# The passage to the experts in another order, with the difference of the first token tile on GpSimd

## The chip, the cores and the metric

The kernel runs on one NeuronCore of a Trainium2 chip. The metric is the device time of one launch in microseconds (us); for the kernel before it is the median of three runs. In the profile PE is TensorE (matmuls; PEld its weight loads), DVE is VectorE, ACT is ScalarE, POOL is GpSimd, and SP is the engine that issues most DMAs.

## What is computed

One layer of an encoder on 256 tokens (and 16 meta tokens) of width 2048, all in float32. The first sub-layer mixes latent attention and retention. The second is a mixture of experts, and the change lies at the passage between the two:

```python
h = layer_norm(ALPHA * h + mix, ln1_g, ln1_b)
g_sel = argmax(h @ w_group + b_group)                     # one of 4 groups
e_local = top_k(e_logits[g_sel] + e_bias, 2)              # two of its 8 experts
e_w = softmax(chosen e_logits) * softmax(g_logits)[g_sel]
y = (silu(x @ w1[e]) * (x @ w3[e])) @ w2[e]               # 32 experts, 512 wide
h = layer_norm(ALPHA * h + sum over the two of e_w * y, ln2_g, ln2_b)
```

## The kernel before

**Precision.** TensorE multiplies float32 at full rate only in a rounded form (float32r). So each operand is kept as a rounded high part and a low part that holds the difference. ScalarE copies a piece of weights (`raw`) to its high part `wh`, VectorE subtracts and writes `wl`. A *unit* is 1 MB of weights (128 partitions by 2048 columns), and the expert weights are 384 units: 12 for each of 32 experts (4 each of w1, w3 and w2). Units x = 10 and 22 of each pair of experts are used unsplit in four-pass float32 (`XR`, line 286).

**Stream of weights.** SP issues the loads into a ring of eight slots (`load`, line 436). The load of unit n waits until TensorE has used unit n - 8. Units 0 to 7 are loaded in the first sub-layer; unit 8 is the first whose load waits for an expert unit.

**The expert loop.** Experts are taken in pairs, 24 steps k to a pair. The first pair leaves out k = 4 to 7 (`body` and `step`, lines 422 to 428), so that its steps are k = 0 to 3 and 8 to 23; its unit at k = 14 is the unsplit one, x = 10. At each step every engine does its part for the unit and then small tasks bound to certain k: ScalarE evicts (`copy_up`, `outputs`, `gathered`), VectorE selects (`select`), builds the next gather matrix and the hidden products, TensorE folds hidden products (`mix`, line 1010, at k = 12, which waits for `s_pd` of `select`). Four gathers of the next pair follow the units k = 8 to 11 of the first pair (`G_FIRST`).

**The passage.** The normalised stream `mrg` (two token tiles t, each 128 tokens by 2048) is split into `xh1` (ScalarE, line 644) and `xl1` (VectorE, `stream_rest`, line 682), and in both the columns are permuted by a strided read, 16 elements apart. `xl1` lies over `yt`, which the router's logits (TensorE, line 2157, banks 0 and 1) read until `s_lg`. From the logits VectorE finds the assignment in some 30 small operations, each waiting for the one before (lines 712 to 733, helper `first_max`). TensorE computes ranks from it (lines 953 to 956), VectorE adds them up to `rk_`, builds the gather matrix `pg` (line 742) and a maximum (`s_mxr`, line 753). TensorE then gathers the tokens of the first two experts: for each of eight blocks q of two column groups, and for the high and the low part h, it multiplies the token tile by `pg` into a PSUM bank (`first_gather`, line 973), and ScalarE evicts each block to `xg` (`gathered`, line 555), in the order of q and after `s_gt` counts q + 1. The units of the first expert need two more blocks at each step.

Between the parts TensorE is fed with idle matmuls (`keep_warm`, line 944): 36 behind the logits, 16 behind the ranks. VectorE's order is written out: assignment, `stream_rest(0)`, ranks, gather matrix, maximum, `stream_rest(1)`, the splits of units 0 to 3 (line 755), then the first pair. At k = 3 VectorE runs all of `combine_weights` (line 758) and ScalarE the exponentials for it (`weights_exp`, line 633); `select` of the first pair is at k = 8. TensorE gathers the high parts of blocks 0 to 5 and the low parts of 0 to 3 ahead of unit 0, blocks 4 and 5 (low part) ahead of k = 1, and blocks 6 and 7 ahead of k = 2, for which banks 7 and 6 must have been evicted.

GpSimd computes inverse roots (line 1768), issues the constants' DMAs, and in the expert loop the scatters of results (`scatter`, line 521), which go through its queue.

Of the kernel before, what the change touches and what calls it, by code (L numbers as in the profile page):

```python
# [5 lines left out]
F32 = mybir.dt.float32  # L6
# [12 lines left out]
TT = SEQ // P  # L19
# [72 lines left out]
def moe_trunk(nc, ins, out):  # L92
# [15 lines left out]
    with ctx:  # L108
# [252 lines left out]
        s_xh1 = sem("s_xh1")  # L361
        s_xl1 = sem("s_xl1")
        s_lg = sem("s_lg")
# [66 lines left out]
        G_AT = (4, 6, 8, 10, 16, 18, 20, 22)  # L430
        FIRST_BANK = (7, 6, 5, 4, 3, 2, 7, 6)
        G_FIRST = (8, 9, 10, 11, 16, 18, 20, 22)
# [87 lines left out]
        def pool_experts(pool):  # L520
            def scatter(filled, par):

                pool.wait_ge(s_h1, TT)
                pool.wait_ge(s_ye[par], filled)
                pool.indirect_dma_start(yscr[:, :], bass.IndirectOffsetOnAxis(dest[0:SLOTS, par:par + 1], 0),  # L525
                                        yall[0:SLOTS, par, :], None, bounds_check=SCRATCH_ROWS - 1,
                                        oob_is_err=False).then_inc(s_scat[par], 16)

            def pairs(first, end):
                with pool.Fori(first, end) as p:  # L530
                    scatter(p, 0)
                    scatter(p, 1)

            pairs(1, PAIRS + 1)
            pool.wait_ge(s_nx, 1)
            more = pool.value_load(nxi[0:1, 0:1], min_val=0, max_val=ROUNDS - 1)
            with pool.If(more > 0):
                pairs(PAIRS + 1, PAIRS * (more + 1) + 1)
            for par in range(2):
                pool.wait_ge(s_scat[par], 16 * PAIRS * (more + 1))  # L540
            nc.gpsimd.tensor_tensor(marks[:, 5:6], half[:, 0:1], half[:, 0:1], ALU.mult).then_inc(s_all, 1)

        def scalar_experts(act):
# [46 lines left out]
            def pair(turn, par, first=False, early=None, last=False):  # L590
                for x in body(first):
# [5 lines left out]
                    hi(turn, x + HELD)  # L597
                    if k == 3 and early:
                        early()
# [62 lines left out]
        def vector_experts(dve, own):  # L662
# [19 lines left out]
            def stream_rest(t):  # L682

                dve.wait_ge(s_xh1, t + 1)
                nc.vector.tensor_tensor(xl1[:, t, :, :], mrg[:, t, :].rearrange("q (p k) -> q k p", k=KD),
                                        xh1[:, t, :, :].bitcast(F32), ALU.subtract).then_inc(s_xl1, 1)

# [46 lines left out]
            dve.wait_ge(s_asg, 1)  # L734
            stream_rest(0)
            own.after(nc.vector.tensor_scalar(r1[:, :, :], asg[:, :, :], -1000.0, 1000.0, ALU.mult, ALU.add))
# [20 lines left out]

            def combine_weights():

# [7 lines left out]
                nc.vector.tensor_tensor(ex[:, :, 0], rs[:, 10:12], rs[:, 14:16], ALU.subtract)  # L767
                nc.vector.tensor_tensor(ex[:, :, 1], rs[:, 12:14], rs[:, 14:16], ALU.subtract).then_inc(s_r1, 1)

                dve.wait_ge(s_mxt, 1)  # L770
# [75 lines left out]
            def pair(turn, p, first=False, early=None, last=False):  # L846
                for x in body(first):
                    k = step(x, first)
                    if k == (8 if first else 5):
                        select(turn, p)  # L850
# [5 lines left out]
                    lo(turn, x + HELD)  # L856
                    if k == 3 and early:
                        early()
                    if k == 0 and not first:
# [20 lines left out]

            one_round(0, 1, early=combine_weights)
            dve.wait_ge(s_nx, 1)
# [57 lines left out]
        def tensor_experts(pe, turn_stream, logits):  # L940
# [8 lines left out]
            for j in range(4):  # L949
                logits(j)  # L950
            keep_warm(36)

# [19 lines left out]

            def first_gather(q, h):

                bank = ps[:, FIRST_BANK[q], :].rearrange("p (k a h s) -> p k a h s", k=2, a=2, h=2)
                for b in range(2):
                    for t in range(TT):
                        m = nc.tensor.matmul(bank[:, b, :, h, :], (xh1, xl1)[h][:, t, 2 * q + b, :],
                                             pg[:, t, :].rearrange("p (a s) -> p a s", a=2),
                                             start=t == 0, stop=t == 1, skip_group_check=True)  # L980
                if h:
                    m.then_inc(s_gt, 1)
# [44 lines left out]
            def pair(turn, par, first=False, early=False, last=False):  # L1027
                for x in body(first):
                    k = step(x, first)
                    j = 2 * turn  # L1030
                    if early and k < 4:
                        if k == 1:
                            first_gather(4, 1)
                            first_gather(5, 1)
                        if k == 2:
                            for q in (6, 7):
                                pe.wait_ge(s_xg, q - 5)
                                first_gather(q, 0)
                                first_gather(q, 1)
                        pe.wait_ge(s_xg, 2 * k + 2)  # L1040
                    elif k == 0:
                        pe.wait_ge(s_xg, 8 * turn + 8)
# [58 lines left out]

            keep_warm(16)
            pe.wait_ge(s_pg, 1)
            pe.wait_ge(s_mxr, 1)
            pe.wait_ge(s_xh1, TT)
            for q in range(6):
                first_gather(q, 0)
            pe.wait_ge(s_xl1, TT)
            for q in range(4):
                first_gather(q, 1)  # L1110
            one_round(0, early=True)
# [1147 lines left out]
```

## Time and profile before

| | |
|---|---|
| median of 3 runs | 2149.41 us (2149.09 to 2151.28) |
| profiled execution, span from the first to the last instruction | 2148.8 us |
| median above that span | 0.6 us |
| PE, DVE, ACT, POOL busy | 96%, 74%, 59%, 5% of the span |
| HBM read | 595.05 MB |
| expert weights, loads of 1 MB by line 450 | 384 |
| mean granted TensorE clock | 0.987 |

Of the profiled execution the profile gives the span alone; what lies around it (start and end of the launch) is inside the 0.6 us by which the median stands above it. The busy shares are averages over two sub-layers with different limits. In the timeline rows below, the first number is the start in us, the second the duration, xN a merged run of N operations, and the bracket at the end the idle time of the engine before it and who ended it. A granted clock (PEclk) of 1.00 is TensorE's 2.4 GHz, 0.50 its 1.2 GHz.

### The profile page before, as it was taken

To read this page: it belongs to the slowest core of one execution; us is meant where nothing else is said; L and a number is where in the kernel's file an instruction comes from. 1 tells how busy PE (TensorE), PEld (TensorE's weight loads), DVE (VectorE), ACT (ScalarE), POOL (GpSimd) and SP (SyncE) were. 2 spreads that over 40 slices of the span, in tenths; PEclk is the share of its full clock that TensorE was granted. 3 is DMA by queue.
4 is the path that set the end of the run, shared out by engine and by line. 5 is a ranking of instruction groups with operands and counts; after the bars stand their busy time and mean duration, and the time that the engine had idled before them with its cause. 6 is when DMAs were issued, how large, how long until landed. Compare 5 with 4: busy or idle time off the path is not lost.

```text
span 2148.8 us, 30033 instructions
## 1 busy us (share of the span) xinstructions
PE 2061.8 (96%) x11484; PEld 1753.2 (82%) x11484; DVE 1596.2 (74%) x1413; ACT 1276.5 (59%) x1060; POOL 106.1 (5%) x77
## 2 busy tenths in 40 slices
PE   8999999999999999999999999999999999999992
PEld 8998888899999998887897778777777777777871
DVE  7646655453737365445668999999999999999997
ACT  5435663333233333333347888888888888888872
POOL 1000000000000000001000000000000000000001
PEclk9999999999999999999999999999999999999996
DMA  6554335655454544557747999999999999999993
GB/s 214 157 138 157 119 128 184 199 180 173 157 161 152 175 154 144 192 195 232 246 196 291 421 421 421 421 421 420 418 420 418 418 421 416 416 415 420 418 409 156
DMA packets 164607, 602.50 MB, mean 280 GB/s; under 512 B 20320, under 2 KB 28656, under 8 KB 113424
## 3 DMA queue, kind: packets, MB, share of 16 engines
q1 hardware_dynamic: 160816, 593.81, 72.7%
q0 software_dynamic: 3712, 7.59, 1.2%
q8 instruction: 55, 0.90, 0.2%
q14 instruction: 24, 0.20, 0.0%
HBM read 595.05 MB, written 18.89 MB: 286 GB/s over the span
## 4 chain that ended last, share of the span: by engine, by line
PE 66%; DVE 16%; issue 7%; DMA 7%; ACT 3%; DVEq 0%; POOLq 0%; POOL 0%; SPq 0%; ACTq 0%
PE ps L1825 19%; PE ps L1806 15%; DVE wl L692 11%; DMA raw<-in_w_dram 7%; PE ps L998 6%; PE ps L999 5%; PE ps L2177 4%; PE ps L995 3%; ACT wh L553 2%; PE ps L1020 2%; PE ps L1931 2%; PE ps L1911 2%; PE ps L1898 1%; DVE yall L843 1%; PE ps L968 1%
## 5 line engine op out<-in xcount | busy, mean ns | idle before, releaser
L692 DVE TENSOR_TENSOR wl<-raw,wh 128x2048 fp32r<-128x2048 f32 x352 | 792.0, 2288 | 42.2 <-ACT wh L553 41.1
L553 ACT ACTIVATE wh<-raw 128x2048 fp32r<-128x2048 f32 x352 | 671.1, 1916 | 140.1 <-DMA raw<-in_w_dram 83.9
L1396 DVE TENSOR_TENSOR wl<-raw,wh 128x2048 fp32r<-128x2048 f32 (+1 forms) x168 | 379.9, 2264 | 283.8 <-ACT wh L1200 283.7
L1200 ACT ACTIVATE wh<-raw 128x2048 fp32r<-128x2048 f32 (+1 forms) x168 | 318.1, 1896 | 443.7 <-DMA raw<-in_w_in_dram 282.2
L998 PE MATMUL ps<-wh,xg 128*128 128x512 f32 x900 | 376.1, 418 | 24.4 <-DVE wl L692 24.1
L999 PE MATMUL ps<-wl,xg 128*128 128x512 f32 x900 | 354.1, 393 | 0.0
L1806 PE MATMUL ps<-hth,wh 128*128 128x272 f32 (+1 forms) x896 | 259.7, 290 | 3.2 <-DVE wl L1396 1.8
L1806 PE MATMUL ps<-htl,wh 128*128 128x272 f32 (+1 forms) x896 | 255.8, 285 | 0.0
L1806 PE MATMUL ps<-hth,wl 128*128 128x272 f32 (+1 forms) x896 | 255.6, 285 | 0.0
L998 PEld LDWEIGHTS ps<-wh,xg 128*128 128x128 f32 x900 | 170.3, 189 | 77.2 <-DVE wl L692 30.3
L998 PE MATMUL ps<-wh,hx 128*128 128x512 f32 x508 | 202.0, 398 | 0.8 <-DVE wl L692 0.8
L999 PEld LDWEIGHTS ps<-wl,xg 128*128 128x128 f32 x900 | 170.5, 189 | 38.8 <-issue 7.4
L999 PE MATMUL ps<-wl,hx 128*128 128x512 f32 x508 | 198.5, 391 | 0.0
L1806 PEld LDWEIGHTS ps<-hth,wh 128*128 128x128 f32 x896 | 168.8, 188 | 5.8 <-DVE wl L1396 2.5
L1806 PEld LDWEIGHTS ps<-htl,wh 128*128 128x128 f32 x896 | 168.7, 188 | 0.3
L1806 PEld LDWEIGHTS ps<-hth,wl 128*128 128x128 f32 x896 | 168.6, 188 | 0.0
L1825 PE MATMUL ps<-wh,hth 128*128 128x512 f32 x384 | 156.1, 406 | 0.0
L1825 PE MATMUL ps<-wh,htl 128*128 128x512 f32 x384 | 151.2, 394 | 0.0
L1825 PE MATMUL ps<-wl,hth 128*128 128x512 f32 x384 | 150.8, 393 | 0.0
L525 POOL DMA_INDIRECT yscr<-yall,dest x32 | 69.4, 2170 | 942.5 <-DVE yall L843 937.9
L998 PEld LDWEIGHTS ps<-wh,hx 128*128 128x128 f32 x508 | 95.6, 188 | 20.2 <-issue 1.6
L995 PE MATMUL ps<-raw,xg 128*128 128x512 f32 x248 | 111.5, 592 | 0.0
(348 smaller groups left out, 3079.2 us busy)
## 6 DMA issues: line engine op xcount, KB each, us to landing
raw<-in_w_dram SPq DMA_DIRECT2D x384, 1024.0 KB, 10.3
raw<-in_w_in_dram SPq DMA_DIRECT2D x103, 1024.0 KB, 5.1
raw<-in_w_pa_dram SPq DMA_DIRECT2D x16, 1024.0 KB, 5.0
raw<-in_w_pb_dram SPq DMA_DIRECT2D x16, 1024.0 KB, 5.0
raw<-in_w_out_dram SPq DMA_DIRECT2D x16, 1024.0 KB, 5.0
raw<-in_w_ukv_dram SPq DMA_DIRECT2D x8, 1024.0 KB, 5.4
yrow<-yscr SPq DMA_DIRECT2D x4, 1024.0 KB, 7.8
raw<-in_w_uq_dram SPq DMA_DIRECT2D x8, 384.0 KB, 3.5
```

The costliest lines, as they stand in the source:

```text
L525: pool.indirect_dma_start(yscr[:, :], bass.IndirectOffsetOnAxis(dest[0:SLOTS, par:par + 1], 0), yall[0:SLOTS, par, :], None, bounds_check= ...
L553: nc.scalar.activation(wh2[:, x % HELD, :], raw2[:, slot2(x), :], ACT.Copy).then_inc(s_wh2, 1)
L692: nc.vector.tensor_tensor(wl2[:, slot2(x), :], raw2[:, slot2(x), :], wh2[:, x % HELD, :].bitcast(F32), ALU.subtract).then_inc(s_wl2, 1)
L995: m = nc.tensor.matmul(o, s.bitcast(F32), raw2[:, slot2(x), c:c + 512], start=st, stop=sp_, skip_group_check=True)
L998: nc.tensor.matmul(o, s, wh2[:, x % HELD, c:c + 512], start=st, stop=False, skip_group_check=True)
L999: m = nc.tensor.matmul(o, s, wl2[:, slot2(x), c:c + 512], start=False, stop=sp_, skip_group_check=True)
L1020: nc.tensor.matmul(ps[:, 6, c:c + SLOTS], ab[:, v, P * f:P * (f + 1)], fold[:, :], start=True, stop=True, skip_group_check=True)
L1200: nc.scalar.activation(wh[:, n % RING1, 0:c], raw1[:, n % RING1, 0:c], ACT.Copy).then_inc(s_wh, 1)
L1396: nc.vector.tensor_tensor(wl[:, n % RING1, 0:c], raw1[:, n % RING1, 0:c], wh[:, n % RING1, 0:c].bitcast(F32), ALU.subtract).then_inc(s_wl, 1)
L1806: m = nc.tensor.matmul(ps[:, bank, col:col + width], w[:, n % RING1, c:c + P], s[:, 4 * u + k, c0:c0 + width], start=opens and u == 0 and ...
L1825: m = nc.tensor.matmul(ps[:, bank + t, :], s[:, 4 * u + k, c:c + P], w[:, n % RING1, 512 * k:512 * (k + 1)], start=u == 0 and k == 0 and j ...
L2177: m = nc.tensor.matmul(ps[:, bank + t, :], s[:, 4 * u + k, P * t:P * (t + 1)], w[:, n % RING1, 512 * k:512 * (k + 1)], start=u == 0 and k ...
```

## The change

Five things are edited. GpSimd makes the difference of token tile 0, once the logits and the tile's high part are there, ahead of its loop of scatters; VectorE no longer does, and the semaphore `s_xl1` becomes one for each tile. The warm-up matmuls are 18 and 3 instead of 36 and 16. The first gather takes seven blocks (bank 1 joins) as one run, first all high parts, then the low parts of tile 0, then those of tile 1, and the eighth block behind them; nothing of it stays between the units. `combine_weights` is cut in two: `exponents` at k = 3 and the rest at k = 10. `select` of the first pair moves from k = 8 to k = 11, and ScalarE's exponentials from k = 3 to k = 9.

```diff
         s_yt = sem("s_yt")
         s_ytc = sem("s_ytc")
         s_xh1 = sem("s_xh1")
-        s_xl1 = sem("s_xl1")
+        s_xl1 = [sem(f"s_xl1_{t}") for t in range(TT)]
         s_lg = sem("s_lg")
         s_r1 = sem("s_r1")
         s_r2 = sem("s_r2")
@@ -428,7 +428,7 @@
             return x if first and x < 4 else x + 4
 
         G_AT = (4, 6, 8, 10, 16, 18, 20, 22)
-        FIRST_BANK = (7, 6, 5, 4, 3, 2, 7, 6)
+        FIRST_BANK = (7, 6, 5, 4, 3, 2, 1, 7)
         G_FIRST = (8, 9, 10, 11, 16, 18, 20, 22)
         LAST_BANK = (0, 1, 6, 7)
 
@@ -531,6 +531,10 @@
                     scatter(p, 0)
                     scatter(p, 1)
 
+            pool.wait_ge(s_lg, 1)
+            pool.wait_ge(s_xh1, 1)
+            nc.gpsimd.tensor_tensor(xl1[:, 0, :, :], mrg[:, 0, :].rearrange("q (p k) -> q k p", k=KD),
+                                    xh1[:, 0, :, :].bitcast(F32), ALU.subtract).then_inc(s_xl1[0], 1)
             pairs(1, PAIRS + 1)
             pool.wait_ge(s_nx, 1)
             more = pool.value_load(nxi[0:1, 0:1], min_val=0, max_val=ROUNDS - 1)
@@ -595,7 +599,7 @@
                     if k == (19 if last else 23):
                         copy_up(turn, x, 2 * turn + 1, 1)
                     hi(turn, x + HELD)
-                    if k == 3 and early:
+                    if k == 9 and early:
                         early()
                     if k == 0 and not first:
                         sigmoid(2 * turn - 1)
@@ -683,7 +687,7 @@
 
                 dve.wait_ge(s_xh1, t + 1)
                 nc.vector.tensor_tensor(xl1[:, t, :, :], mrg[:, t, :].rearrange("q (p k) -> q k p", k=KD),
-                                        xh1[:, t, :, :].bitcast(F32), ALU.subtract).then_inc(s_xl1, 1)
+                                        xh1[:, t, :, :].bitcast(F32), ALU.subtract).then_inc(s_xl1[t], 1)
 
             def lo(turn, x):
                 if x % 24 in XR:
@@ -732,7 +736,6 @@
 
             nc.vector.tensor_tensor(asg[:, :, :], oh1[:, :, :], oh2[:, :, :], ALU.add).then_inc(s_asg, 1)
             dve.wait_ge(s_asg, 1)
-            stream_rest(0)
             own.after(nc.vector.tensor_scalar(r1[:, :, :], asg[:, :, :], -1000.0, 1000.0, ALU.mult, ALU.add))
             dve.wait_ge(s_rank, 1)
             pr = ps[:, 6:8, 0:E]
@@ -755,7 +758,7 @@
             for x in range(HELD):
                 lo(0, x)
 
-            def combine_weights():
+            def exponents():
 
                 own.after(nc.vector.tensor_reduce(rs[:, 2:4], gl, AXX, ALU.max))
                 nc.vector.tensor_tensor(eg[:, :, :], gl, b3(rs[:, 2:4], G), ALU.subtract).then_inc(s_r1, 1)
@@ -766,6 +769,8 @@
                 own.after(nc.vector.tensor_tensor(rs[:, 14:16], rs[:, 10:12], rs[:, 12:14], ALU.max))
                 nc.vector.tensor_tensor(ex[:, :, 0], rs[:, 10:12], rs[:, 14:16], ALU.subtract)
                 nc.vector.tensor_tensor(ex[:, :, 1], rs[:, 12:14], rs[:, 14:16], ALU.subtract).then_inc(s_r1, 1)
+
+            def combine_weights():
 
                 dve.wait_ge(s_mxt, 1)
                 own.after(nc.vector.tensor_reduce(nxf[:, 0:1], ps[0:1, 5, 0:P], AXX, ALU.max))
@@ -846,7 +851,7 @@
             def pair(turn, p, first=False, early=None, last=False):
                 for x in body(first):
                     k = step(x, first)
-                    if k == (8 if first else 5):
+                    if k == (11 if first else 5):
                         select(turn, p)
                     if k == 0 and first:
                         gather_matrix(turn + 1, 2 * p + 2)
@@ -854,8 +859,8 @@
                         product(2 * turn + 1, 1, turn)
                         hidden_split(2 * turn + 1, hx2)
                     lo(turn, x + HELD)
-                    if k == 3 and early:
-                        early()
+                    if k in (3, 10) and early:
+                        early[k == 10]()
                     if k == 0 and not first:
                         hidden(2 * turn - 1, 1, turn - 1)
                     if k == 1 and not first and not last:
@@ -878,7 +883,7 @@
                 pair(turn + PAIRS - 1, PAIRS - 1, last=True)
                 last_rest(turn + PAIRS - 1, rounds)
 
-            one_round(0, 1, early=combine_weights)
+            one_round(0, 1, early=(exponents, combine_weights))
             dve.wait_ge(s_nx, 1)
             more = dve.value_load(nxi[0:1, 0:1], min_val=0, max_val=ROUNDS - 1)
             with dve.If(more > 0):
@@ -948,7 +953,7 @@
 
             for j in range(4):
                 logits(j)
-            keep_warm(36)
+            keep_warm(18)
 
             pe.wait_ge(s_asg, 1)
             nc.tensor.matmul(ps[:, 6, 0:N_EXP], before[:, :], asg[:, 0, :], start=True, stop=True)
@@ -970,15 +975,15 @@
                                                  start=t == 0, stop=t == 1, skip_group_check=True)
                 m.then_inc(s_gt, 1)
 
-            def first_gather(q, h):
+            def first_gather(q, h, tiles_):
 
                 bank = ps[:, FIRST_BANK[q], :].rearrange("p (k a h s) -> p k a h s", k=2, a=2, h=2)
                 for b in range(2):
-                    for t in range(TT):
+                    for t in tiles_:
                         m = nc.tensor.matmul(bank[:, b, :, h, :], (xh1, xl1)[h][:, t, 2 * q + b, :],
                                              pg[:, t, :].rearrange("p (a s) -> p a s", a=2),
                                              start=t == 0, stop=t == 1, skip_group_check=True)
-                if h:
+                if h and tiles_[-1] == TT - 1:
                     m.then_inc(s_gt, 1)
 
             def unit(turn, x, pairs_, start, stop):
@@ -1029,14 +1034,6 @@
                     k = step(x, first)
                     j = 2 * turn
                     if early and k < 4:
-                        if k == 1:
-                            first_gather(4, 1)
-                            first_gather(5, 1)
-                        if k == 2:
-                            for q in (6, 7):
-                                pe.wait_ge(s_xg, q - 5)
-                                first_gather(q, 0)
-                                first_gather(q, 1)
                         pe.wait_ge(s_xg, 2 * k + 2)
                     elif k == 0:
                         pe.wait_ge(s_xg, 8 * turn + 8)
@@ -1099,15 +1096,19 @@
                 for par in range(2):
                     pe.wait_ge(s_ye[par], last + 1)
 
-            keep_warm(16)
+            keep_warm(3)
             pe.wait_ge(s_pg, 1)
             pe.wait_ge(s_mxr, 1)
             pe.wait_ge(s_xh1, TT)
-            for q in range(6):
-                first_gather(q, 0)
-            pe.wait_ge(s_xl1, TT)
-            for q in range(4):
-                first_gather(q, 1)
+            for q in range(7):
+                first_gather(q, 0, (0, 1))
+            for t in range(TT):
+                pe.wait_ge(s_xl1[t], 1)
+                for q in range(7):
+                    first_gather(q, 1, (t,))
+            pe.wait_ge(s_xg, 1)
+            for h in range(2):
+                first_gather(7, h, (0, 1))
             one_round(0, early=True)
             more = pe.value_load(nxi[0:1, 0:1], min_val=0, max_val=ROUNDS - 1)
             with pe.If(more > 0):

```

## Rows read from the trace of the kernel before

**Rows 1.** Busy time by windows, expert loop: window, length, busy us (count) by engine, clock, DMA.

```profile
core 0: us, PE busy (x) PEld busy (x) DVE busy (x) ACT busy (x) POOL busy (x), PEclk, DMA share, GB/s
...
1300.00:1400.00 100.00, 97.93 (x492) 78.66 (x491) 96.46 (x65) 85.29 (x65) 9.01 (x4) 1.00 1.01 421
```

**Rows 2.** The same view, four windows of the passage.

```profile
1152.00:1154.00 2.00, 2.00 (x11) 1.81 (x12) 1.86 (x6) 2.00 (x3) 0.00 (x0) 0.74 0.26 107
1154.00:1156.00 2.00, 2.00 (x6) 1.52 (x6) 2.00 (x2) 0.60 (x2) 0.00 (x0) 0.50 0.00 0
1156.00:1158.00 2.00, 2.00 (x14) 1.77 (x13) 1.73 (x1) 1.47 (x2) 0.00 (x0) 0.90 0.30 49
1164.00:1166.00 2.00, 2.00 (x6) 0.89 (x5) 1.18 (x5) 1.89 (x1) 0.00 (x0) 1.00 0.59 127
```

**Rows 3.** Timeline of TensorE, first expert pair: start, duration, operation, idle before it.

```profile
1151.96 0.41 PE L968 MATMUL ps<-pg,xh 128*128 128x128 f32 x2 [3.77 <-ACT xg L558]
...
1159.57 1.97 PE L1020 MATMUL ps<-fold,ab 128*128 128x64 f32 x16 [0.31 <-ACT xg L558]
...
1163.72 3.59 PE L995 MATMUL ps<-raw,xg 128*128 128x512 f32 x8
```

**Rows 4.** Timeline of VectorE, the passage.

```profile
1115.63 0.22 DVE L733 TENSOR_TENSOR asg<-oh,oh 128x64 f32<-128x64 f32 x1
1115.89 3.75 DVE L685 TENSOR_TENSOR xl<-mrg,xh 128x2048 fp32r<-128x2048 f32 x1
...
1121.41 0.23 DVE L739 TENSOR_TENSOR rk__152<-ps,r 128x64 f32<-128x64 f32 x1 [1.67 <-PE ps L956]
...
1122.47 0.22 DVE L753 TENSOR_REDUCE rs<-r 128x1 f32<-128x64 f32 x1
...
1126.23 8.89 DVE L692 TENSOR_TENSOR wl<-raw,wh 128x2048 fp32r<-128x2048 f32 x4
...
1138.27 8.90 DVE L692 TENSOR_TENSOR wl<-raw,wh 128x2048 fp32r<-128x2048 f32 x4 [2.01 <-ACT wh L553]
1147.09 0.15 DVE L760 TENSOR_REDUCE rs<-lg 128x2 f32<-128x8 f32 x1
...
1153.17 0.17 DVE L802 COPY wdc<-wd 128x8 f32<-128x8 f32 x1
```

**Rows 5.** Timeline of TensorE, the passage.

```profile
1109.70 11.01 PE L947 MATMUL ps<-ident,ones 128*128 128x128 f32 x72
...
1121.14 3.82 PE L947 MATMUL ps<-ident,ones 128*128 128x128 f32 x32
...
1127.43 1.95 PE L978 MATMUL ps<-pg,xl 128*128 128x128 f32 x16
...
1131.17 1.00 PE L978 MATMUL ps<-pg,xl 128*128 128x128 f32 x8
1132.01 0.44 PE L998 MATMUL ps<-wh,xg 128*128 128x512 f32 x1
```

**Rows 6.** Warm-up line alone, 1109.6 to 1115 us: durations min/median/max, first and last start.

```profile
L947 PE MATMUL ps<-ident,ones x25: 421/421/561, 1109.7 to 1115.0; 128*128 128x128 f32 x25
```

**Rows 7.** Timeline of ScalarE, the passage.

```profile
1107.83 7.35 ACT L644 ACTIVATE xh<-mrg 128x2048 fp32r<-128x2048 f32 x2 [2.40 <-DVE mrg L679]
...
1136.33 7.31 ACT L553 ACTIVATE wh<-raw 128x2048 fp32r<-128x2048 f32 x4
```

**Rows 8.** Timeline of GpSimd: inverse roots twice, first scatter of the expert loop.

```profile
554.69 2.70 POOL L1768 TENSOR_TENSOR rstd<-var,half 128x2 f32<-128x2 f32 x1 [541.65 <-DVE var L1627]
562.87 0.70 POOL L1768 TENSOR_TENSOR rstd<-var,half 128x2 f32<-128x2 f32 x1 [5.47 <-DVE var L1627]
...
1185.97 2.28 POOL L525 DMA_INDIRECT yscr<-yall,dest  x1 [84.49 <-DVE yall L843]
```

**Rows 9.** Timeline of VectorE beside those three.

```profile
554.54 2.29 DVE L1396 TENSOR_TENSOR wl<-raw,wh 128x2048 fp32r<-128x2048 f32 x1
...
562.79 0.99 DVE L1634 TENSOR_SCALAR onat<-ps,gmv,rstd 128x256 f32<-128x256 f32 x2
...
1185.08 4.49 DVE L692 TENSOR_TENSOR wl<-raw,wh 128x2048 fp32r<-128x2048 f32 x2
```

## The prediction, made before the change was timed

> **What bounds the kernel now.** Start with the windows of the expert loop. There the DMA engines are busy the whole time at 421 GB/s, and TensorE and VectorE run at 98 and 96% beside them [rows 1]; the next six windows of 100 us read 416 to 420. The stream of expert weights (384 loads of 1 MB) sets the pace there, so what the passage before it costs is carried to the end as a shift, until the last moment at which the DMA engines wait for a free slot. The windows of the passage show these moments: nothing moves at 1154 to 1156, and a load's worth is missing at 1164 to 1166 [rows 2]. A load is issued when the unit eight places before it has been used. The last gap is that before load 18, which waits for the raw unit (k = 14) of the first pair: that unit starts at 1163.72 and its matmuls take 3.59, so it ends at 1167.3 [rows 3]. A load needs 2.5 (1.05 MB at 421 GB/s), and the units behind this one are used faster than that, so the queue stays full. **The forecast is how far this 1167.3 moves.**
>
> What sets it? The timeline of TensorE: the mix of the hidden products starts at 1159.57; ahead of it TensorE stood still for 3.77 us up to 1151.96, because ScalarE, holding the next xg eviction, sat in the exponentials, which waited for VectorE [rows 3]. VectorE's timeline behind it: assignment at 1115.63 to 1115.85, the difference of tile 0 (3.75), then 1.67 idle until TensorE's rank matmuls, whose result is read at 1121.41; 1.28 later (1122.69) the ranks and the maximum are out, tile 1's difference follows, four splits (8.89), four more (8.90) from 1138.27, the combine weights from 1147.09, and selection until 1153.34 [rows 4]. Why are the rank matmuls so late? TensorE is in 72 warm-up passes (36 matmuls of two) from 1109.70 to 1120.7 [rows 5]. Half of that time is at the granted half clock: 25 passes between 1109.7 and 1115.0, 0.21 apart, against 3.82 for 32 (0.114 apart) later [rows 5, 6].
>
> **The change, part by part.** *18 instead of 36 warm-ups*: 36 passes; 26 at 0.214 to 1115.3 and ten at 0.11 end at 1116.4. With the assignment at 1115.9 the ranks could start 4.2 us sooner. *3 instead of 16* behind the ranks: 26 passes, nothing by itself, since TensorE then waits for the maximum; it costs nothing if the clock holds.
>
> *Tile 0's difference leaves VectorE* (3.75 saved, of which 1.67 was cover for the warm-ups) *and goes to GpSimd*. That starts when ScalarE's first xh1 copy is done: 1107.83 + 7.35/2 = 1111.5 [rows 7]; the logits, which it waits for too, are done where the warm-ups start. No row prices a column of such a subtraction on GpSimd. Lower bound: VectorE's own time for the same strided tile, 3.75 [rows 4]. Upper: ScalarE's pass with one input takes 3.68 [rows 7]; two reads and the write, one after another, are 11.0, say 11.2. I take two reads in turn with the write beside them, 7.4, because GpSimd's reads in this trace behave as through one door (next). The Trainium skill gives 4.5 us for a contiguous subtraction-like pass of 2048 columns (GPSIMD Engine Reference, 3.1); times this kernel's ratio of strided to plain on VectorE, 3.75/2.28, that would be 7.4 as well, an estimate.
>
> *What it collides with.* This decides the case. GpSimd's power of two columns takes 0.70 us at 562.87, beside a VectorE operation that reads PSUM, and 2.70 at 554.69, beside a VectorE subtraction of two SBUF tensors begun at 554.54 for 2.29: it waited 2.0, until 556.8, and then ran its 0.70 [rows 8, 9]. The scatter issue at 1185.97 takes 2.28 the same way. So the two engines exclude each other where both read SBUF. Here GpSimd starts at 1111.5 in the middle of the router's chain, 30-odd small VectorE operations with pauses between them and half of them with two SBUF inputs, which ends at 1115.85. I take it that GpSimd gets in at the first pause (1111.6) and the next two-input operation (1111.88) stands until it has finished. The trace shows only VectorE holding up GpSimd, not the reverse.
>
> The Trainium skill has the rule for both directions (SBUF — State Buffer, Who interferes with whom): the pair is an exclusive lock, and whoever issues second is blocked for the other's whole instruction. By it the chain stands for the whole GpSimd pass; the trace agrees in the one direction, with its 2.0 us.
>
> *The sum, pass 7.4.* GpSimd until 1119.0; the chain is 7.1 late, assignment at 1123.0. Rank matmuls (0.85 from their start at 1120.56 to the read before, 0.2 more at half clock), 1.28 to the maximum: 1125.4, where before it was 1122.69. Tile 1's difference until 1129.1. TensorE has stood since 1116.4, and I take it to be at half clock until some 5 us after it restarts at 1123.1 (as it was after 1109.7): of 28 gathers of high parts from 1125.5, 13 take 0.21 and 15 take 0.113, until 1130.0; the low parts of tile 0 and tile 1 (14 each) and the eighth block (8 matmuls) end at 1134.1. Unit 0 takes 1.85 (1129.3 to 1131.17 before [rows 5]) and ends at 1136.0, 4.9 later than before. ScalarE converts unit 4 behind it in 7.31/4 [rows 7], until 1137.9. VectorE's first four splits are done at 1137.9, the next gather matrix (0.4) at 1138.3, the next four splits at 1147.2, where before they ended at 1147.1: up to here the change has won nothing. Then the *split of the early work* pays: the 6.25 of exponents, weights and selection (1147.09 to 1153.34 before [rows 4]) with two splits (4.45) between them end at 1157.9, on VectorE without a pause. TensorE, with eight more units of 1.85 and four gathers of 0.86 (1131.17 to 1132.01 before, and here as there), has used unit 8 at 1154.2. The mix is at 1158.0, where before it was at 1159.57. **1.6 us are gained.** The exponentials move behind k = 9, where ScalarE has the slack; the gathers of k = 10 and 11 wait for nothing new. *Bank 1 and the seven-block order* make all gathers one piece ahead of unit 0 rather than between units: the 24 matmuls are moved, not added; the eighth block waits for one eviction, which is over while the other six blocks are still being finished.
>
> *The clock again.* TensorE now stands 3.8 us ahead of the mix (1154.2 to 1158.0); before, 3.77 us of standing [rows 3] were followed by the half clock: 0.74, 0.50 and 0.90 granted in three windows [rows 2] are 1.04 + 2.0 + 0.4 = 3.4 us of it, which cost 1.7. The fall moves from k = 10 to the mix, where it lies on the path and no split of VectorE's covers it any more: I charge it, 1.7. **Sum: -1.6 + 1.7 = +0.1.**
>
> GpSimd's scatter (first at 1185.97) is far behind its new work; SP's queue has the same loads, with load 8 4.9 us later, covered by the slack until load 17. The splitting of the semaphore costs nothing. The profiled span is 2148.8, and 0.6 under the median of the runs; on the median the forecast is 2149.41 + 0.1 = 2149.5.
>
> **Rivals.**
> *A, no lock against VectorE*: GpSimd's reads give way, or slip between. For it: from 1185.08 VectorE's two splits took 4.49, no more than others [rows 9], though GpSimd was at work beside it. Against: an address list is little to read. Then the assignment is ready at 1115.9, maximum 1118.5, unit 0 ends at 1127.8, splits at 1140.4, selection at 1151.1: the mix 8.5 earlier, less 1.7 for the clock: 2142.6.
> *B, GpSimd becomes the bound, slower than before*: everything above shifts one for one with the pass, so with a pass of P us the result is P - 7.3 against before: nil at 7.3, over 0.2% at 11.6. At the upper bound of 11.2: +3.9, 2153.3. For it: GpSimd is slow in all its rows, and strides hurt; against: nothing prices it.
> *C, the change doesn't relieve VectorE*: the chain keeps the door, GpSimd gets in at 1115.9 and holds back the gather matrix (two SBUF inputs) until 1123.3; maximum at 1124.2, 1.2 earlier than in the sum: 2148.3.
> *No second fall of the clock* within the forecast: 2147.8.
>
> **How the numbers follow.** Forecast 0.50, A 0.22, B 0.20, C 0.08. A measurement of this kernel can tell about 0.2%, 4.3 us, from no change. Faster by more: A, and the edge of the forecast with the pass at 3.7 and no fall of the clock (5.3 gained, 2144.1): 0.27. Slower by more: the upper part of B, 0.13. The rest, 0.60. The range takes in A (2142.6) and the upper bound of the pass (2153.3): 2142.3 to 2153.6. The forecast alone, with a pass of 6 to 8.5 and the clock's 1.7 or not, reaches from 2146.4 to 2150.6.
>
> **What will show it.** A VectorE operation of the router with some 7 us instead of 0.2, or a gap as long, while GpSimd runs; assignment near 1123; a half clock in the gathers; unit 0 ending near 1136; the mix near 1158. If no router operation is lengthened, A holds. If GpSimd's pass is over 9 us, B. If the loop's DMA share falls below 1, the shift isn't carried, and the whole reckoning falls.

## The result, and the profile after

The changed kernel took 2158.87 us (median of 5 runs, 2156.93 to 2162.55) against 2149.41 (2149.09 to 2151.28) before: 1.0041 times as long, 95% interval 1.0030 to 1.0051. It is slower by some 9 us, outside the range of the forecast (2142.3 to 2153.6). The profiled execution is the slowest of the five, 2162.55 us with a span of 2160.7.

The slowing arises in the passage. The first scatter of the expert loop stood at 1185.97 before [rows 8]; the last but two ran at 2066.26. After, the two are at 1195.29 and 2074.99, 9.3 and 8.7 us later: the loop carries the shift nearly unchanged. (What the profiled run lost beyond it, it lost in the last pair, where a granted clock of 0.59 stands from 2080 to 2090; so the single run is 2 to 3 us above what the passage explains.)

GpSimd's new pass (the timeline of GpSimd, after):

```profile
1112.60 5.57 POOL L536 TENSOR_TENSOR xl<-mrg,xh 128x2048 fp32r<-128x2048 f32 x1 [10.26 <-ACT xh L648]
1195.29 2.29 POOL L525 DMA_INDIRECT yscr<-yall,dest  x1 [77.13 <-DVE yall L848]
```

VectorE beside it (its timeline, after; compare [rows 4]):

```profile
1112.64 0.16 DVE L708 TENSOR_REDUCE rs<-r 128x2 f32<-128x8 f32 x1
1112.83 5.35 DVE L709 TENSOR_TENSOR r<-r,rs 128x8 f32<-128x8 f32 x1
1118.22 0.17 DVE L710 SCALAR_TENSOR_TENSOR r<-r,order 128x8 f32<-128x8 f32 x1
...
1122.37 0.22 DVE L737 TENSOR_TENSOR asg<-oh,oh 128x64 f32<-128x64 f32 x1
...
1124.24 0.23 DVE L742 TENSOR_TENSOR rk__152<-ps,r 128x64 f32<-128x64 f32 x1 [1.42 <-PE ps L961]
...
1125.31 0.22 DVE L756 TENSOR_REDUCE rs<-r 128x1 f32<-128x64 f32 x1
...
1164.33 0.16 DVE L807 COPY wdc<-wd 128x8 f32<-128x8 f32 x1
```

The comparison of eight columns at 1112.83, a matter of 0.17 us, took 5.35 and ended 0.01 us behind GpSimd's pass. So the lock works in this direction too. (The reduction at 1112.64, with one input, began 0.04 us behind GpSimd's start and kept its 0.16.) The assignment comes at 1122.4. This was forecast, and with 5.57 the pass was even cheaper than the 7.4 I took. Now TensorE (its timeline, after; compare [rows 3, 5]):

```profile
1111.30 6.25 PE L952 MATMUL ps<-ident,ones 128*128 128x128 f32 x36
1122.65 0.64 PE L959 MATMUL ps<-asg,before 128*128 128x32 f32 x2 [5.09 <-DVE asg L737]
...
1123.95 1.63 PE L952 MATMUL ps<-ident,ones 128*128 128x128 f32 x6
1125.63 6.21 PE L983 MATMUL ps<-pg,xh 128*128 128x128 f32 x28
1131.63 6.17 PE L983 MATMUL ps<-pg,xl 128*128 128x128 f32 x28
...
1139.31 0.73 PE L1003 MATMUL ps<-wh,xg 128*128 128x512 f32 x1
...
1164.75 3.64 PE L1025 MATMUL ps<-fold,ab 128*128 128x64 f32 x16 [3.43 <-DVE wdc L807]
...
1172.56 4.07 PE L1000 MATMUL ps<-raw,xg 128*128 128x512 f32 x8
```

TensorE stands for 5.09 us ahead of the ranks. From there on each gather takes 0.21: the 64 matmuls from 1125.63 to 1139.31 need 13.7 us, where at the full clock's 0.113 they would need 7.2. The windows (length, busy time and count of each engine, then the clock, the DMA share and GB/s) show how long it stays so:

```profile
1122.00:1132.00 10.00, 9.31 (x42) 9.04 (x43) 8.37 (x12) 0.00 (x0) 0.00 (x0) 0.52 0.00 0
1132.00:1142.00 10.00, 10.00 (x43) 9.42 (x43) 6.36 (x4) 4.13 (x8) 0.00 (x0) 0.50 0.00 0
1164.00:1174.00 10.00, 9.25 (x31) 7.75 (x32) 6.49 (x10) 2.15 (x3) 0.00 (x0) 0.52 0.40 153
```

0.52 and 0.50 belong to 20.5 us at 1.2 GHz in all (summed over windows of 1 us from 1122 to 1143). The stretch begins at 1122.3, in the last moments of the stand, and from 1122.65 on TensorE was busy all that time. A second one of 10.2 us, from 1163.3 to 1173.5, begins within the stand of 3.43 ahead of the mix. Before, the only one between the ranks and the raw unit was 3.4 us long [rows 2].

### The profile page after: what moved, and what is told of

The parts are those of the page before. It is cut to its first block, busy times and chain, and to the rows that moved or that the text cites. A ratio compares the mean times of both kernels' runs of the same rounds, so it can differ in the third digit from the quotient of the medians.

```text
span 2160.7 us, 29909 instructions
## 1 busy us (share of the span) xinstructions
PE 2070.5 (96%) x11422; PEld 1760.2 (81%) x11422; DVE 1596.9 (74%) x1412; ACT 1274.5 (59%) x1060; POOL 111.8 (5%) x78
## 4 chain that ended last, share of the span: by engine, by line
PE 65%; DVE 18%; issue 7%; DMA 6%; ACT 3%; DVEq 0%; POOLq 0%; POOL 0%; SPq 0%; ACTq 0%
PE ps L1826 19%; PE ps L1807 15%; DVE wl L696 12%; DMA raw<-in_w_dram 6%; PE ps L1003 6%; PE ps L1004 5%; PE ps L2178 4%; PE ps L1000 3%; ACT wh L557 2%; PE ps L1025 2%; PE ps L1932 2%; PE ps L1912 2%; PE ps L1899 1%; DVE yall L848 1%; PE ps L973 1%
## 5 line engine op out<-in xcount | busy, mean ns | idle before, releaser
L1003 PEld LDWEIGHTS ps<-wh,xg 128*128 128x128 f32 x900 | 171.2, 190 | 75.5 <-DVE wl L696 28.2
## 6 DMA issues: line engine op xcount, KB each, us to landing
raw<-in_w_dram SPq DMA_DIRECT2D x384, 1024.0 KB, 10.2
```

Of the source, the lines that this page charges most:

```text
L1003: nc.tensor.matmul(o, s, wh2[:, x % HELD, c:c + 512], start=st, stop=False, skip_group_check=True)
```

## The experiments

Each of the eleven was timed beside the kernel before on the same chip, in 6 to 12 runs each (the kernel before had a median of 2151.0 to 2151.8 us there, with single runs from 2148.4 to 2156.9). Two readings of each profiled run go beside the time: how long the passage lasts, from VectorE's first operation on the logits (`lraw`) to the first scatter (76.0 us before, 83.8 after), and the time at half clock between the ranks and unit 0 ("gathers"), and around the mix. The start of the passage itself wavers by 1.4 us from run to run (9.2 to 10.6 behind the first pass over the stream); the logits run partly at half clock in every version, in stretches of 6.8 or 10.2 us that begin anywhere from 1103.9 to 1106.6. The column "passage" leaves this start out. It is one execution for each version, and two executions of the same code can differ by more than a microsecond (see e4_warm_mix below).

| run | what it is | ratio to before (95%) | passage | half clock: gathers | mix |
|---|---|---|---|---|---|
| before | | 1 | 76.0 | 0 | 3.4 |
| the change | | 1.0041 (1.0030 to 1.0051) | 83.8 | 20.5 | 10.2 |
| e1_warm | change, 36 and 16 warm-ups | 1.0011 (1.0002 to 1.0020) | 78.8 | 3.4 | 10.2 |
| e8_long_first | change, 36 and 3 | 1.0030 (1.0019 to 1.0041) | 82.1 | 17.1 | 6.8 |
| e8_long_second | change, 18 and 16 | 1.0016 (1.0007 to 1.0024) | 78.7 | 6.8 | 6.8 |
| e2_no_pool | change without GpSimd's part | 1.0023 (1.0014 to 1.0032) | 79.2 | 17.1 | 6.8 |
| e2w_no_pool_warm | the same, 36 and 16 | 0.9996 (0.9987 to 1.0004) | 75.3 | 0 | 10.2 |
| e3_pool_only | before, GpSimd's part alone | 1.0012 (1.0002 to 1.0022) | 76.4 | 0 | 3.4 |
| e9_before_short | before, 18 and 3 | 1.0021 (1.0012 to 1.0030) | 79.0 | 13.6 | 6.8 |
| e7_pool_late | e1_warm, GpSimd behind the assignment | 1.0005 (0.9996 to 1.0014) | 75.5 | 0 | 10.2 |
| e10_write_only | e1_warm, GpSimd only writes | 1.0000 (0.9991 to 1.0009) | 75.2 | 0 | 10.3 |
| e4_warm_mix | e1_warm, 14 warm-ups at the mix | 0.9995 (0.9986 to 1.0003) | 72.9 | 0 | 0 |
| e6_no_pool_warm_mix | e2w, 14 warm-ups at the mix | 0.9968 (0.9957 to 0.9980) | 71.4 | 0 | 0 |

### The warm-ups or the lock? Each undone alone

e1_warm: the changed kernel with

```diff
-            keep_warm(18)
+            keep_warm(36)
...
-            keep_warm(3)
+            keep_warm(16)
```

> The changed kernel with the old counts of warm-ups, 36 and 16, and nothing else undone. Theory C (the clock): TensorE stood for 5 us while GpSimd held VectorE, restarted at half clock and stayed there for 20 us, through all 64 gathers and unit 0; with the longer warm-ups it stands for under 2 us, the gathers run 0.11 apart, unit 0 ends some 6 us sooner, and the time is about 2152.5 (2151 to 2154.5). Theory L (the lock alone): the loss is the 5.35 us for which a VectorE operation stood, and warm-ups change nothing: 2158 to 2160.

0.30% of the 0.41% went: 1.0011 times before. The chain is held just as long, yet TensorE's timeline and windows are these:

```profile
1111.44 9.58 PE L952 MATMUL ps<-ident,ones 128*128 128x128 f32 x72
1122.89 0.41 PE L959 MATMUL ps<-asg,before 128*128 128x32 f32 x2 [1.88 <-DVE asg L737]
...
1123.59 5.44 PE L952 MATMUL ps<-ident,ones 128*128 128x128 f32 x32
1128.79 3.32 PE L983 MATMUL ps<-pg,xh 128*128 128x128 f32 x28
```

```profile
1122.00:1132.00 10.00, 9.11 (x67) 9.11 (x68) 8.97 (x13) 0.00 (x0) 0.00 (x0) 0.83 0.01 2
1132.00:1142.00 10.00, 10.00 (x64) 8.95 (x64) 7.74 (x5) 7.91 (x11) 0.00 (x0) 1.00 0.30 102
1164.00:1174.00 10.00, 10.00 (x28) 6.62 (x29) 4.06 (x8) 4.41 (x4) 0.00 (x0) 0.76 0.43 131
```

The stand is 1.88 us. The clock still falls, but rises again while the 32 passes of the second warm-up run, and 28 gathers take 3.3 us instead of 6.2. Theory C holds. A rest of 0.11% stays; how much of it is GpSimd's pass, the next but one run tells.

e2_no_pool: the changed kernel without the GpSimd operation and its two waits, and with

```diff
             dve.wait_ge(s_asg, 1)
+            stream_rest(0)
```

> The changed kernel with tile 0's difference back on VectorE behind the assignment, warm-ups 18 and 3 as changed. Theory C: TensorE still stands for some 3.5 us between the ranks and the maximum; if that is enough for the half clock, the gathers crawl again, unit 0 ends near 1138 and the time is about 2155; if not, unit 0 ends at 1130.5 and the time is 2147 to 2148. Theory L: the maximum is 3.6 us sooner than in the changed kernel, and that is all: 2155, with or without a half clock in the gathers. The trace's granted clock tells which.

1.0023 times before. The assignment is ready 5.2 us sooner in the passage (5.65 us behind its start, as before), and still the gathers crawl: TensorE stands 3.56 us between ranks and gathers, and 17.1 us at half clock follow:

```profile
1117.51 0.41 PE L956 MATMUL ps<-asg,before 128*128 128x32 f32 x2 [0.38 <-DVE asg L733]
...
1118.20 0.91 PE L949 MATMUL ps<-ident,ones 128*128 128x128 f32 x6
1122.67 6.20 PE L980 MATMUL ps<-pg,xh 128*128 128x128 f32 x28 [3.56 <-DVE pg L747]
```

So the half clock doesn't need GpSimd's lock. Both theories had a sum of 2155 here, and only the granted clock tells them apart, in favour of C.

e2w_no_pool_warm: both edits together. 

> The changed kernel without the GpSimd edit and with 36 and 16 warm-ups: the reordered gathers and the divided early work alone. Theory C: no half clock in the gathers; unit 0 ends about 1134 (3 later than before, since all gathers stand ahead of it), the early work in two parts wins 3.8 at the mix, the fall of the clock ahead of the mix gives back 1.7 to 3.7: 2147 to 2150. Theory L (only the lock makes the change slow): all of the reordering's gain shows, 2145 to 2146.

0.9996 (0.9987 to 1.0004): no difference that can be measured. The mix comes 5.5 us sooner after the start of the passage than before (44.1 for 49.6), but its half clock of 10.2 us for 3.4 takes nearly all of it back: 75.3 against 76.0 at the scatter. The fold of the mix and the raw unit show it:

```profile
1154.23 3.64 PE L1022 MATMUL ps<-fold,ab 128*128 128x64 f32 x16 [3.43 <-DVE wdc L804]
...
1162.04 4.69 PE L997 MATMUL ps<-raw,xg 128*128 128x512 f32 x8
```

The outcome is C's, and L's 2145 to 2146 didn't come. Against e1_warm (1.0011) the run puts GpSimd's pass at 0.15%; the two intervals just overlap.

e3_pool_only: the kernel before, with GpSimd's operation ahead of its scatters, `stream_rest(0)` taken from VectorE and a semaphore for each tile. 

> The kernel before with the GpSimd edit alone (tile 0's difference there, a semaphore for each tile); order and warm-ups as before. The router's chain stands 5.3 us longer, 3.75 us of VectorE's work and 1.67 us of its idle time are saved. Theory C: the warm-ups reach to 1120.6, TensorE stands for under 1 us, no half clock in the gathers, +0.9: 2150.3 (2149 to 2151.5). Theory L: the same sum if the lock's cost is netted, 5.3 or more on top if it isn't: 2154 to 2155.

1.0012 (1.0002 to 1.0022); passage 76.4, 0.4 longer. By the trace the netted sum is right (0.9 forecast): 36 warm-ups cover most of the held chain, the first gathers run at full clock. The ratio allows up to 4.7 us, so it doesn't exclude that something of the lock shows beyond that.

e9_before_short: the kernel before, with 18 for 36 and 3 for 16 warm-ups. 

> The kernel before with 18 and 3 warm-ups and nothing else changed. Theory W: the ranks come 1.6 us sooner, TensorE then stands 3.5 us until the maximum, the clock falls, and the 40 gathers ahead of unit 0 and unit 0 itself run at half clock: unit 0 ends 2 to 3 us later, 0.05 to 0.15% above before. Theory without the clock: 1.6 us sooner throughout, 0.07% under before.

1.0021 (1.0012 to 1.0030): half of the whole loss from two constants, with no other edit. The direction is W's, the size is larger (0.05 to 0.15% forecast): 13.6 us at half clock through the 40 gathers and unit 0, and 6.8 for 3.4 later. The first 24 gathers, in the kernel before and then in e9:

```profile
1124.72 2.88 PE L978 MATMUL ps<-pg,xh 128*128 128x128 f32 x24
```

```profile
1122.90 5.36 PE L978 MATMUL ps<-pg,xh 128*128 128x128 f32 x24 [3.56 <-DVE pg L747]
```

The theory without the clock falls.

### What brings the clock back

e8_long_first and e8_long_second restore one count each.

```diff
# e8_long_first
-            keep_warm(18)
+            keep_warm(36)
# e8_long_second
-            keep_warm(3)
+            keep_warm(16)
```

> The changed kernel with 36 warm-ups ahead of the ranks but 3 behind them. In e1_warm the clock fell behind a stand of 1.9 us too, and rose again within 3 us while the 16 second warm-ups ran. Theory W (the clock rises while warm-ups run, and does not rise while the gathers run): here the gathers follow at once, at half clock to their end, and the time is near that of the changed kernel, 0.35 to 0.45% above before. Theory S (the length of the stand decides): 1.9 instead of 5.1 us of standing, gathers mostly at full clock, 0.1 to 0.2% above before.

> The changed kernel with 18 warm-ups ahead of the ranks and 16 behind them: TensorE stands 5.1 us and restarts at half clock. Theory W: the clock rises during the 32 passes or at their end, the gathers run 0.11 apart, the passes at half clock hold them up by 2 to 3 us against e1_warm: 0.15 to 0.25% above before. Theory S: gathers at half clock as in the changed kernel, and later still: 0.45 to 0.55% above before.

1.0030 and 1.0016. The second alone does nearly as much as both (1.0011), the first alone little. (The interval of e8_long_first, 1.0019 to 1.0041, just touches theory S's 0.1 to 0.2%; the traces decide.) The timelines of TensorE, first of e8_long_first, then of e8_long_second:

```profile
1122.82 0.41 PE L959 MATMUL ps<-asg,before 128*128 128x32 f32 x2 [1.70 <-DVE asg L737]
...
1123.52 0.91 PE L952 MATMUL ps<-ident,ones 128*128 128x128 f32 x6
1125.16 6.21 PE L983 MATMUL ps<-pg,xh 128*128 128x128 f32 x28 [0.73 <-DVE pg L750]
```

```profile
1121.31 0.64 PE L959 MATMUL ps<-asg,before 128*128 128x32 f32 x2 [6.12 <-DVE asg L737]
...
1122.62 5.80 PE L952 MATMUL ps<-ident,ones 128*128 128x128 f32 x32
1128.17 3.32 PE L983 MATMUL ps<-pg,xh 128*128 128x128 f32 x28
```

With a stand of 1.70 us and 6 passes behind it the gathers run at half clock to their end (6.21 for 28). With a stand of 6.12 us and 32 passes they run at full (3.32), although TensorE stood longer. So the length of the stand doesn't decide (theory S falls); what ran after it does: the clock rose while the warm-ups ran in both kernels in which it had fallen there and 32 passes followed (e1, e8_long_second), and it never rose during the gathers of the four kernels that had only 6 passes (the change, e2, e8_long_first, e9), in up to 13.7 us of unbroken work.

### The second stretch, at the mix

```diff
                     if k == 12:
+                        if early:
+                            keep_warm(14)
                         mix(...)
```

in e1_warm gives e4_warm_mix, in e2w_no_pool_warm e6_no_pool_warm_mix.

> The changed kernel with 36 and 16 warm-ups (as e1_warm) and 14 more ahead of the first pair's mix, where TensorE stood 3.4 us and then ran 10 us at half clock. Theory C2 (this second half-clock stretch lies on the path): mix, unit 9 and the raw unit at full clock end 3.7 us sooner than in e1_warm, which was 0.11% above the kernel before: 0.05 to 0.1% under it now. Theory Q (the full queue of loads behind it hides the stretch): as e1_warm, +0.11%.

> No GpSimd edit, 36 and 16 warm-ups, and 14 more ahead of the first mix: the version that should be the fastest. Theory C2: 4 us under e2w_no_pool_warm (0.04% under before), so 0.18 to 0.27% under the kernel before. Theory Q: no different from e2w_no_pool_warm.

0.9995 (0.9986 to 1.0003), from 1.0011, and 0.9968 (0.9957 to 0.9980), from 0.9996. In both the stretch is gone and the time with it, so the queue of loads doesn't hide it (theory Q falls). Timeline of TensorE, e6_no_pool_warm_mix:

```profile
1152.78 3.29 PE L949 MATMUL ps<-ident,ones 128*128 128x128 f32 x28
1156.37 1.97 PE L1022 MATMUL ps<-fold,ab 128*128 128x64 f32 x16 [0.31 <-DVE wdc L804]
...
1160.53 3.59 PE L997 MATMUL ps<-raw,xg 128*128 128x512 f32 x8
```

The mix takes 1.97 instead of 3.64 in e2w, and from its start to the end of the raw unit 7.7 us pass instead of 12.5. The 14 warm-ups themselves fall into the stand that was there. e6 is the fastest version tried: 2145.03 us against 2151.80 of the kernel before beside it, 6.8 us less, and faster than both kernels. The forecast for it was 0.18 to 0.27% under before; it is 0.32%.

Not all of the 5.8 us by which e4's passage is shorter than e1_warm's comes from the mix. Up to there the two kernels are the same code, and yet e1 had 3.4 us at half clock behind the ranks and e4 none:

```profile
1121.26 0.41 PE L959 MATMUL ps<-asg,before 128*128 128x32 f32 x2 [2.13 <-DVE asg L737]
```

The stand of 2.13 us was followed by no fall here (nor was that of 2.15 in e3), that of 1.88 in e1 was. The mix of e4 starts 1.6 us sooner in the passage than that of e1; the other 4.2 us are the mix's and the two units' behind it. What makes one execution fall and not the other is open.

### What exactly is held

e7_pool_late: e1_warm, with GpSimd's first wait changed.

```diff
-            pool.wait_ge(s_lg, 1)
+            pool.wait_ge(s_asg, 1)
```

> As e1_warm (36 and 16 warm-ups), but GpSimd's pass over tile 0 waits for the assignment, so that it runs beside the warm-ups and VectorE's idle time instead of within the router's chain. Theory K (the lock costs what stands behind the held operation): the chain is as quick as before, GpSimd works from about 1116 to 1121.6, VectorE has next to nothing with two SBUF inputs to do until the gather matrix at 1121.9; 4.9 us sooner than e1_warm at the maximum, and the time is that of e2w_no_pool_warm, 0 to 0.1% under before. Theory N (a GpSimd pass costs its length wherever it stands): as e1_warm, 0.1% above before.

1.0005 (0.9996 to 1.0014), passage 75.5 instead of 78.8. The interval takes in both forecasts, K's 0.9996 and N's 1.0011; the traces have to tell. GpSimd's pass and VectorE's timeline beside it:

```profile
1117.73 5.55 POOL L536 TENSOR_TENSOR xl<-mrg,xh 128x2048 fp32r<-128x2048 f32 x1 [15.72 <-DVE asg L737]
```

```profile
1117.69 0.20 DVE L739 TENSOR_SCALAR r<-asg 128x64 f32<-128x64 f32 x1
1121.94 0.23 DVE L742 TENSOR_TENSOR rk__152<-ps,r 128x64 f32<-128x64 f32 x1 [4.06 <-PE ps L961]
1122.20 1.11 DVE L743 TENSOR_SCALAR rk__152<-rk__152 128x4 f32<-128x4 f32 x1
1123.35 0.43 DVE L750 TENSOR_TENSOR pg<-slots,rk__152 128x256 fp32r<-128x256 f32 x1
```

The chain is as short as before (assignment at 5.65 us of the passage), and the ranks' sum at 1121.94, which reads one operand from PSUM, passes beside GpSimd. The operation at 1122.20 doesn't: 1.11 instead of 0.17, until 1123.31, when GpSimd's pass is over (1123.28). It is a TENSOR_SCALAR with a single SBUF tensor. I had looked for the lock at operations with two SBUF inputs only. The Trainium skill counts it among the operations that can contend with GpSimd when their operands meet certain conditions (SBUF — State Buffer, Who interferes with whom). This case agrees, with 0.9 us of waiting. Theory K holds by the trace: what the pass costs depends on what stands behind the held operation.

e10_write_only: e1_warm with a fill in the place of the subtraction; the low part of tile 0 is left out of the computation.

```diff
-            nc.gpsimd.tensor_tensor(xl1[:, 0, :, :], mrg..., xh1..., ALU.subtract)
+            nc.gpsimd.memset(xl1[:, 0, :, :].bitcast(F32), 0.0)
```

> As e1_warm, but GpSimd only fills tile 0's low part with zeros, reading nothing from SBUF: the difference of tile 0 is left out, which changes no instruction's count or order elsewhere. Theory R (the two engines exclude each other by their reads): no operation of the router's chain is lengthened, the assignment is ready near 1116, the time is 0 to 0.1% under before. Theory G (any GpSimd pass of that size holds VectorE): an operation of the chain stands as long as the fill takes, and the assignment is late by that.

```profile
1111.97 1.81 POOL L536 MEMSET xl<- 128x2048 f32 x1 [10.24 <-ACT xh L647]
```

```profile
1112.49 0.17 DVE L726 TENSOR_TENSOR r<-lg,brt 128x8 f32<-128x8 f32 x1
1112.69 0.16 DVE L707 TENSOR_REDUCE rs<-r 128x2 f32<-128x8 f32 x1
1112.89 0.17 DVE L708 TENSOR_TENSOR r<-r,rs 128x8 f32<-128x8 f32 x1
1113.09 0.17 DVE L709 SCALAR_TENSOR_TENSOR r<-r,order 128x8 f32<-128x8 f32 x1
```

During the fill of 1.81 us the small operations of VectorE, some with two SBUF inputs, keep their usual 0.16 and 0.17, and the assignment is ready at 5.65 us of the passage, as before. The time is 1.0000 times before. Theory G falls, and this is what R expected. That it is the missing read is the likeliest account, but it isn't shown by itself: the fill is also another operation, and a third as long.

## Why the prediction was wrong

**The bound, the anchor: right.** The loop carries the shift: 9.3 us at the first scatter, 8.7 at the last but two, with the DMA share at 1.01 throughout.

**The lock, both ways: right.** Held: one two-input operation, to within 0.01 us of GpSimd's end. I gave this 0.50 and its absence (rival A) 0.22; A fell. The pass was 5.57, within the bounds (3.75 to 11.2) and 1.8 under the value taken; the estimate with VectorE's ratio of strided to plain was too high, and rival B fell with it: the kernel is slower, but not by a long pass. The chain came 5.2 us late instead of 7.1. Rival C fell too: GpSimd got in at once.

**The step that failed: "I take it to be at half clock until some 5 us after it restarts at 1123.1 (as it was after 1109.7)".** The clock stayed down 20.5 us. The row I took it from was one of warm-up passes, and in the changed kernel what followed was gathers, which behave otherwise (e8_long_first against e8_long_second). It was also only the tail of a stretch. Of these windows of the kernel before the first two show that the clock fell at 1105.2, with the logits' matmuls running and TensorE busy throughout, and the third that it rose within 1115 to 1116, after 10.2 us and not 5:

```profile
1104.00:1105.00 1.00, 1.00 (x12) 1.00 (x11) 1.00 (x1) 1.00 (x1) 0.00 (x0) 1.00 1.00 418
1105.00:1106.00 1.00, 1.00 (x8) 1.00 (x7) 0.96 (x2) 0.43 (x1) 0.00 (x0) 0.60 0.99 418
...
1115.00:1116.00 1.00, 1.00 (x9) 1.00 (x9) 0.86 (x5) 1.00 (x2) 0.00 (x0) 0.78 0.00 0
```

By this step the 64 gathers and unit 0 took 13.7 and 3.5 us; I had 8.6 and 1.85. That is 6.8 us, the larger part of the miss. It is also why "3 instead of 16 ... costs nothing if the clock holds" went wrong: the condition was named and then not priced.

**Mis-sized: the second fall.** Forecast at the mix, at the right place, charged with 1.7 from the row of before. Measured 11.9 us from the start of the mix to the end of the raw unit (1164.75 to 1176.6), where full clock takes 7.7: 4.1. Again the row came from a place where other work followed the stand, eight gathers and one unit there, the mix and one unit here, and the stretch was 3.4 us long there and 10.2 here. Why the second was longer is not shown.

**The sum, remade.** With the pass as measured, the forecast's own steps give -3.5 at the mix (-1.6 and 1.9 less of waiting) and 1.7 for the clock: -1.8. Add 6.8 for the gathers and unit 0, 2.4 for the second fall and 0.5 for ranks at half clock (2.9 us from assignment to maximum, 2.4 forecast): +7.9 at the end of the raw unit (and of this +3.8 at the mix, where the trace has +3.6). The passage is 7.8 us longer in the trace, and the runs are 9 us slower, with an interval of 6 to 11. The overestimate of the pass hid 1.9 us of the two errors of the clock.

**By edit**, from the ratios: the short warm-ups 0.30% (the change less e1), GpSimd's pass 0.15% (e1 less e2w), the new order with the early work in two 0.04% to the good (e2w), within the noise. From the passages: 5.0, 3.5 and -0.7 us. These shares depend on what stands beside: the short warm-ups cost 0.21% in the kernel before (e9) and 0.27% without GpSimd's part (e2 less e2w), GpSimd's pass 0.12% (e3), 0.18% (the change less e2) and 0.27% (e4 less e6).

**The early work in two parts: right, but given back.** It brings the mix forward by 5.5 us in e2w (together with the new order of the gathers; no run separates the two). Only e4 and e6 keep a gain, since in the others TensorE then stands ahead of the mix and the clock falls there.

## What to carry to other kernels

Idle matmuls that cover a wait are part of the path behind them: before shortening them, ask what TensorE stands for, and above all whether what it does next brings the clock back. A price for the half clock may be taken only from a whole stretch, with the same work in it. Work moved to GpSimd is free only where VectorE meanwhile has no operation of the kinds held here (two SBUF inputs, or a TENSOR_SCALAR) with work waiting behind it: ahead of a serial chain of small operations a pass of 5.6 us delays the chain by nearly its length, behind that chain next to nothing.

## What the runs showed of the hardware

- GpSimd subtracts 128x2048 float32 with one operand 16 elements apart in 5.55 to 5.59 us (seven runs), where VectorE needs 3.62 to 3.75; a fill of the same size takes 1.81.
- VectorE and GpSimd exclude each other in both directions: 5.35 us for an operation of 0.17. A TENSOR_SCALAR with one SBUF tensor was held like an operation with two (0.94 us, e7); an operation with one input in PSUM and one in SBUF (e7, 1121.94) and a reduction (the change, 1112.64) passed, and GpSimd's fill held none (e10).
- TensorE at half clock: stretches of 3.4 and 6.8 us ended while warm-ups ran (e1, e8_long_second), that of 20.5 us ended 3.5 us after unit 0 had begun (in e2, e8_long_first and e9 it was 2.0, 3.0 and 3.6), and none while the first gathers ran. In e8_long_first the clock fell at 1124.7, in the second of two stands of 1.70 and 0.73 us; in e3 and e4 none followed a stand of 2.15 and 2.13. In all versions it fell once with no stand at all, under the logits' matmuls (1105.2 before).
- What it is about the gathers that doesn't bring the clock back stays open; nothing of them was varied by itself.
